# One-hot rows of the retrieval layer: second key index by one comparison for 8 tokens, gate moved to the first index

## What is computed

```
q = (hf @ wq).reshape(n, 8, 2, 64)
s = einsum('nhpd,hpkd->nhpk', q, subkeys)            # 8 heads, 2 halves, 128 keys each
sv, si = top_k(s, 16)
cand = sv[:, :, 0, :, None] + sv[:, :, 1, None, :]   # 16 x 16 sums per head
top_v, top_pos = top_k(cand, 16)
experts = si0 * 128 + si1 at top_pos                 # 8 x 16 = 128 experts of 16384 per token
gates = softmax(top_v)
act = gelu(einsum('td,tkd->tk', xb, u[experts]))
y = einsum('tk,tkd->td', gates * act, v[experts])
```

## Time and profile before

| what | value |
|---|---|
| median of 3 runs | 3950.86 us (3949.44 to 3951.46) |
| profiled execution, span from first to last instruction | 3944.0 us |
| busy: PE / PE weight load / DVE / ACT / POOL | 3668.8 / 2099.9 / 2582.7 / 732.8 / 1645.1 us |
| granted TensorE clock, mean | 0.972 |

### The profile page before, as it was taken

One profiled execution on the slowest core, in us unless ns is written; L12 is line 12 of the kernel. 1 busy time (PEld: TensorE's weight loads), 2 busy tenths in 40 slices (PEclk: granted clock), 3 DMA queues, 4 the chain that ended last, 5 costly groups with the idle time before them and its releaser, 6 DMA issues. The chain is left out here.

```text
span 3944.0 us, 39966 instructions
## 1 busy us (share of the span) xinstructions
PE 3668.8 (93%) x13726; PEld 2099.9 (53%) x13726; DVE 2582.7 (65%) x5929; ACT 732.8 (19%) x1622; POOL 1645.1 (42%) x1498
## 2 busy tenths in 40 slices
PE   2988888999999999999989887889999999999997
PEld 1545676655555555555445566765555555555543
DVE  5685688777666666677724738878677646556344
ACT  1143355400000000000012535552000000000000
POOL 0030155446556644444502003544777655445340
PEclk7998999999999999999999998999999999999999
DMA  6321234579999999999930131447999999989774
GB/s 218 126 101 46 90 86 145 185 289 405 379 379 369 378 373 378 379 372 353 393 138 2 47 121 54 126 136 256 359 410 410 387 354 354 366 337 359 304 290 160
DMA packets 365386, 1026.96 MB, mean 260 GB/s; under 512 B 30849, under 2 KB 132481, under 8 KB 364417
## 3 DMA queue, kind: packets, MB, share of 16 engines
q0 software_dynamic: 147456, 536.94, 35.5%
q1 hardware_dynamic: 118000, 433.99, 28.9%
q10 hardware_dynamic: 99728, 53.48, 4.8%
HBM read 965.07 MB, written 59.22 MB: 260 GB/s over the span
## 5 line engine op out<-in xcount | busy, mean ns | idle before, releaser
L1859 PE MATMUL ps<-colsT,arena 128*128 128x384 f32 x4096 | 1359.0, 486 | 5.6 <-DMA arena<-in_peer_ut 5.6
L1859 PEld LDWEIGHTS ps<-colsT,arena 128*128 128x128 f32 x4096 | 775.8, 190 | 584.4 <-issue 94.7
L1894 PE MATMUL ps<-arena 128*128 128x512 f32 x1536 | 676.5, 592 | 0.0
L1366 POOL DMA_INDIRECT proj<-in_peer_u,eidx x336 | 478.9, 1425 | 240.9 <-DVE modbc L1560 110.5
L1366 POOL DMA_INDIRECT proj<-in_peer_v,eidx x335 | 361.1, 1078 | 312.7 <-DVE colsT L1571 214.5
L1894 PEld LDWEIGHTS ps<-arena 128*128 128x128 f32 x1536 | 291.8, 190 | 345.2 <-issue 317.6
L1352 POOL TENSOR_SCALAR x<-iota,modbc 128x128 f32<-128x128 f32 x192 | 145.2, 771 | 719.3 <-ACT modbc L1692 551.5
L1560 DVE CUSTOM_DVE_ANT_0 proj<-proj,rows 128x1024 f32<-128x1024 f32 x336 | 399.4, 1222 | 59.0 <-DMA proj<-in_peer_u,eidx 57.2
L1571 DVE SCALAR_TENSOR_TENSOR colsT<-proj,modbc,colsT 128x1024 f32<-128x1024 f32 x330 | 410.1, 1286 | 14.4 <-DMA proj<-in_peer_v,eidx 13.1
L1894 PE MATMUL ps<-arena,rows 128*128 128x512 f32 x768 | 337.8, 592 | 0.0
L1894 PE MATMUL ps<-arena,x 128*128 128x512 f32 x768 | 337.7, 592 | 0.0
(11 more groups left out here) (298 smaller groups left out, 3716.3 us busy)
## 6 DMA issues: line engine op xcount, KB each, us to landing
arena<-in_peer_ut SPq DMA_DIRECT2D x256, 512.0 KB
arena<-in_peer_v SPq DMA_DIRECT2D x256, 512.0 KB
gmat_d<-arena ACTq DMA_DIRECT2D x24, 2048.0 KB, 9.3
arena<-gmat_d SPq DMA_DIRECT2D x64, 768.0 KB
proj<-in_w_adaT SPq DMA_DIRECT2D x48, 512.0 KB
modbc<-in_w_adaT SPq DMA_DIRECT2D x30, 512.0 KB, 3.7
rows<-in_w_adaT SPq DMA_DIRECT2D x18, 512.0 KB, 3.5
arena<-in_w_in SPq DMA_DIRECT2D x2, 4224.0 KB, 16.6
```

The lines of the kernel that those rows point to most:

```text
L1366: pool.indirect_dma_start(ring[slots[at]], None, tab, bass.IndirectOffsetOnAxis(ap=eidx[:, b * SLOTS + q:b * SLOTS + q + 1], axis=0)).then ...
L1859: mm = pe.matmul(ps[:, 2 + j % 2, 0:ND], utab[:, j % UR, k], hT[:, k, NG:T], start=(k == 0), stop=(k == KT - 1))
L1894: mm = pe.matmul(ps[:, Y_BANKS[2 * d + c2], :], wT[j % CR][:, d * P:(d + 1) * P], vtab[:, j % VR, c2 * 512:(c2 + 1) * 512], start=(j == 0) ...
```

## The change

B is made by one tensor_tensor per 8 tokens (iota against j, both broadcast, is_equal), without the gate. The gate goes into A: on POOL the tensor_scalar becomes (iota equal i) times gate, with two per-partition scalars; on ACT the Abs gets scale -1 and the Relu becomes four instructions of 128 columns, relu(gate - 2|i - iota|), because its bias now differs per token. `turned_out` is one instruction of 384 columns and a wait of ACT for its own result. The waits count in sets of 8 tokens.

```
-                        pool.tensor_scalar(agrp[n % A_GRP][:, t], iota128[:, :], ijgT[:, d % 2, 0, 4 * q + t:4 * q + t + 1], 0.0,
-                                           ALU.add, ALU.is_equal).then_inc(p_made, 1)
+                        tok = 4 * q + t
+                        pool.tensor_scalar(agrp[n % A_GRP][:, t], iota128[:, :], ijgT[:, d % 2, 0, tok:tok + 1],
+                                           ijgT[:, d % 2, 2, tok:tok + 1], ALU.is_equal, ALU.mult).then_inc(p_made, 1)
...
-                    for t in range(16 * step, 16 * step + 16):
+                    for t in range(16 * step, 16 * step + 16, B_SET):
                         n = d * P + t
-                        if n >= B_TOK and t % 4 == 0:
-                            dve.wait_ge(g_mm, (n - B_TOK) // 4 + 1)
-                        dve.tensor_scalar(bring[:, n % B_TOK], iota128[:, :], ijgT[:, d % 2, 1, t:t + 1],
-                                          ijgT[:, d % 2, 2, t:t + 1], ALU.is_equal, ALU.mult).then_inc(b_made, 1)
+                        if n >= B_TOK:
+                            dve.wait_ge(g_mm, (n - B_TOK + B_SET) // 4)
+                        dve.tensor_tensor(bring[:, n % B_TOK:n % B_TOK + B_SET],
+                                          iota128[:, :].unsqueeze(1).to_broadcast([P, B_SET, NKEY]),
+                                          ijgT[:, d % 2, 1, t:t + B_SET].unsqueeze(2).to_broadcast([P, B_SET, NKEY]),
+                                          ALU.is_equal).then_inc(b_made, 1)
...
-                    c.link(act.activation(ijgT[:, d % 2, 0], ps[:, 0, 0:P], ACT.Copy, scale=-1.0))
-                    act.activation(ijgT[:, d % 2, 1:3].rearrange("p a t -> p (a t)"), ps[:, 0, P:3 * P], ACT.Copy).then_inc(tr_out, 1)
+                    act.activation(ijgT[:, d % 2].rearrange("p a t -> p (a t)"), ps[:, 0, 0:3 * P], ACT.Copy).then_inc(tr_out, 1)
+                    act.wait_ge(tr_out, d + 1)
...
                     for t in range(4):
-                        c.done(act.activation(four[:, t], iota128[:, :], ACT.Abs, bias=ijgT[:, d % 2, 0, 4 * q + t:4 * q + t + 1]))
+                        tok = 4 * q + t
+                        c.done(act.activation(four[:, t], iota128[:, :], ACT.Abs, scale=-1.0, bias=ijgT[:, d % 2, 0, tok:tok + 1]))
                     c.wait()
-                    act.activation(four, four, ACT.Relu, scale=-1.0, bias=1.0).then_inc(a_made, 1)
+                    for t in range(4):
+                        tok = 4 * q + t
+                        act.activation(four[:, t], four[:, t], ACT.Relu, scale=-2.0,
+                                       bias=ijgT[:, d % 2, 2, tok:tok + 1]).then_inc(a_made, 1)
...
                         if act_marks(n):
-                            pe.wait_ge(a_made, n // 2 + 1)
+                            pe.wait_ge(a_made, 4 * (n // 2) + 4)
...
-                        pe.wait_ge(b_made, 4 * n + 4)
+                        pe.wait_ge(b_made, 4 * n // B_SET + 1)
```

More of the change, by code:

```diff
@@ L43 @@
 UR, VR, GR = 3, 3, 3
-A_GRP, B_TOK = 4, 16
+A_GRP, B_TOK, B_SET = 4, 16, 8
 ADA_RING = 5
@@ L1688, in turned_out @@
                     if d >= 2:
-                        act.wait_ge(b_made, (d - 1) * P)
+                        act.wait_ge(b_made, (d - 1) * (P // B_SET))
                         act.wait_ge(p_made, (d - 1) * (P // 2))
-                    c.link(act.activation(ijgT[:, d % 2, 0], ps[:, 0, 0:P], ACT.Copy, scale=-1.0))
-                    act.activation(ijgT[:, d % 2, 1:3].rearrange("p a t -> p (a t)"), ps[:, 0, P:3 * P], ACT.Copy).then_inc(tr_out, 1)
+                    act.activation(ijgT[:, d % 2].rearrange("p a t -> p (a t)"), ps[:, 0, 0:3 * P], ACT.Copy).then_inc(tr_out, 1)
+                    act.wait_ge(tr_out, d + 1)
                 def mark_rows(n):
```

## The result

| what | before | after |
|---|---|---|
| median of 4 runs | 3950.15 us (3945.36 to 3951.46) | 4005.41 us (3998.52 to 4009.72) |
| ratio, with its 95% interval | | 1.0138 (1.0124 to 1.0152) |
| profiled execution: its span | 3944.0 us | 4003.3 us (its time 4005.1) |
| busy PE / DVE / ACT / POOL | 3668.8 / 2582.7 / 732.8 / 1645.1 us | 3695.2 / 2484.4 / 793.6 / 1722.1 us |
| granted clock, mean | 0.972 | 0.965 |

The change costs 55 us. I had forecast 33 and slower, with 4005 inside the range. The direction holds; 22 us are missing from the sum.

A forecast was written before the change was run, and what follows sets the result against it. The dense loop is TensorE's, and the head's idle time there is mainly ScalarE's chain. Relus add 16.6 us a layer, 33 in two, other terms about 0: 3950.9 + 33 = 3984 us, range 3962 to 4020.

The forecast's parts named there:

- The gap is ScalarE's chain: PE's 1.18 us idle before group 3, steps 1 to 6: ended by ScalarE's mark between two copies, not VectorE.
- B by sets: VectorE making B by sets of 8: 98 us less VectorE work, 0 on the path.
- Relu by token: 0.62 per mark: ScalarE's four Relus for one: 0.62 us more per mark; blocks 6.4, 5.1, 5.1; 33 in two layers.
- POOL's second scalar: POOL's rows of A with one pointer more: taken as 0, bounds 0.71 to 0.85 us a row.
- POOL held by the sets: At a block's start VectorE's sets delay POOL's group 3 rows to 587.6, ScalarE's chain allows 587.4: tie, 0.
- The clock: Rival: gaps grown to 1.8 us lower PE's clock in half of 36 steps, 32 us more, 4016; chance 0.14.
- POOL's two signs: Expected signs: POOL's L1352 mean above 0.85 us, and no PE wait on it in steps 1 to 6.
- The sum's base: Profiled span 3944.0 plus 33 is 3977; median stands 6.9 above the span, so 3950.9 plus 33 is 3984.

The follow-up runs named there:

- after, again: The changed kernel itself, unaltered, run again beside the other kernels: 4002.99 us, ratio 1.0136.
- Relu by token, alone: Kernel before with only its Relu cut into four of 128 columns, each with a per-partition bias: 3993.12 us, ratio 1.0117.
- four Relus, immediate bias: Kernel before with its Relu cut into four of 128 columns, the bias an immediate: 3962.30 us, ratio 1.0039.
- sets alone: Kernel before with only B made by sets of 8 tokens, the gate left out altogether: 3955.63 us, ratio 1.0017.
- after, one Relu: Changed kernel with one 512-column Relu with immediate bias again, even groups without gate; POOL's second scalar kept: 3959.98 us, ratio 1.0033.
- before, marks later: Kernel before with ScalarE's mark of group n + 4 moved behind the copy of group n + 1: 3915.21 us, ratio 0.9918.
- after, marks later: Changed kernel with ScalarE's mark of group n + 4 moved behind the copy of group n + 1: 3956.40 us, ratio 1.0021.
- before, marks later, square first: Kernel before with marks behind copies and `square` and `root` ahead of the mark in block 1: 3908.24 us, ratio 0.9896.
- after, marks later, square first: Changed kernel with marks behind copies and `square` and `root` ahead of the mark in block 1: 3947.30 us, ratio 0.9998.

## Why the prediction was right, and where its size was off

PE in the six blocks of both layers, worked out from the views by stretch of each profile (length, busy, the rest) and, in the last column, from the granted clock: (1 - mean) / 0.5 of the length is the time at 1.2 GHz. The stretches end some 0.2 us later in each layer than those above. Each row is one execution; the changed kernel's two differ by 4 us in busy time and 10 in the last column.

```
kernel                          length   busy   idle   at 1.2 GHz, us
before                           573.8  479.9   93.9   72
after                            625.4  498.1  127.3  113
after, again                     628.6  502.5  126.2  123
Relu by token, alone             615.0  489.9  125.1   96
four Relus, immediate bias       584.8  477.9  106.8   61
sets alone                       581.2  481.4   99.8   75
after, one Relu                  586.7  483.5  103.2   82
before, marks later              540.2  474.3   65.9   75
after, marks later               583.6  486.0   97.6  102
before, marks later, square first 531.2  472.7   58.5   72
after, marks later, square first  572.5  484.0   88.5   89
```

The split has a limit. A run of matmuls counts as busy to its modelled end, so work cut into more runs counts as longer: at a block's start groups 0 and 1 now run apart, 2.05 and 2.08 us for the 3.75 of the earlier trace rows, some 2 us of the 18 in six blocks; and two runs of eight at 1.13 became one of sixteen at 2.02 where the marks stand later.

- *The gap is ScalarE's chain.* Right, and shown three ways: it grew by what the Relus' handing on grew (0.64 and 0.27), taking 98 us of work off VectorE left it at 1.18, and moving the mark closed it.
- *B by sets: 98 us, 0 on the path.* Right. VectorE's wait for exps at the end of block 2 grew as its cover, from 6.45 us to 8.12:

```profile
697.16 0.29 DVE L1453 TENSOR_REDUCE proj<-proj 128x8 f32<-128x128 f32 x1 [8.12 <-ACT proj L1679]
```

- *Relu by token: 0.62 per mark; blocks 6.4, 5.1, 5.1.* Right in size: 0.64, and idle time per block 5.9, 5.3, 5.6. An operand per partition costs 93 ns here (390 against 297). The Trainium skill (ScalarE: Activation LUTs, section "What ACT_TABLE_LOAD costs") has the same 93 ns, and its figures had given 0.65 per mark. That the idle time of the whole change is 33.4 against the sum's 33 is in part luck. The Relus alone give 31.2. The sets with POOL's second scalar, which the sum had at 0, give 9.3 by themselves (103.2 less 93.9), and on top of the Relus only 2.2, which fits the start of a block, where the longer marks and POOL's rows run beside each other.
- *POOL's second scalar: taken as 0.* Wrong, inside its bounds. Four rows beside nothing last 3.11 us after, 0.78 each, where the same view before has 2.80 to 2.95, some 0.70 to 0.74. It is 0.04 to 0.08 a row.
- *POOL held by the sets: a tie, 0.* The mechanism is right, the tie was lost by 0.9 us a start. I had counted two holds in the first eight rows; there are three. Start of block 2, POOL, VectorE, PE and ACT, against the earlier trace rows:

```profile
592.41 0.33 PE L1876 MATMUL ps<-ident,proj 128*128 128x128 f32 x1 [1.82 <-DVEq L1458]
...
593.52 2.36 DVE L1521 TENSOR_TENSOR x<-iota,modbc 128x1024 f32<-128x1024 f32 x2 [1.22 <-ACT modbc L1694]
...
593.59 5.20 POOL L1353 TENSOR_SCALAR x<-iota,modbc 128x128 f32<-128x128 f32 x4 [12.46 <-ACT modbc L1694]
...
598.77 4.16 POOL L1353 TENSOR_SCALAR modbc<-iota,modbc 128x128 f32<-128x128 f32 x4
...
598.84 2.08 PE L1892 MATMUL ps<-x 128*128 128x128 f32 x8 [0.58 <-POOL x L1353]
...
601.03 1.24 DVE L1521 TENSOR_TENSOR x<-iota,modbc 128x1024 f32<-128x1024 f32 x1 [2.04 <-PE ps L1892]
601.45 0.57 ACT L1723 ACTIVATE arena<-ps 128x512 f32<-128x512 f32 x1
...
602.99 1.33 PEld L1892 LDWEIGHTS ps<-x,modbc 128*128 128x128 f32 x8 [0.66 <-POOL modbc L1353]
```

  Here the label is right: POOL's second four end at 602.93 and PE's weight load goes at 602.99. ScalarE's copy of group 1 ended at 602.02, 0.9 earlier and 9.6 after the turn, which is what my chain gave (9.7). The rows 5.20 and 4.16 are 2.09 and 1.05 over the undisturbed 3.11: two holds, and a third from the set at 601.03. Group 3 starts some 10.6 us after the turn, 8.3 before. By the experiments this term, the second scalar, the new `turned_out` and what hangs on them are the 11 us of the changed kernel with one Relu.
- *The clock: taken as 0, and as a rival of 0.14 at 4016.* **This is the term that failed.** PE's busy time rose by 18.2 us, and the clock of all first-layer blocks fell by more than the 0.02 that I had named as the sign of it (the second layer's by 0.02, 0.01 and 0). The time at 1.2 GHz rose by 41 us, and at half speed that can add some 20 to the busy time. Two rows of block 2 after, scores and a group, timeline of PE:

```profile
617.10 3.52 PE L1853 MATMUL ps<-proj 64*128 64x128 f32 x32
...
658.29 1.96 PE L1892 MATMUL ps<-x,modbc 128*128 128x128 f32 x8 [1.82 <-POOL x L1353]
```

  The scores take 2.06 us at the full clock, the eight matmuls 1.13. Both rows stand just behind a gap of 1.82. Busy time by stretch, block 2 from 25 us behind its turn to its end, the kernel before and the kernel after:

```profile
602.72:672.06 69.34, 60.30 (x324) 43.78 (x324) 56.38 (x235) 38.40 (x86) 33.78 (x40) 1.00 0.58 171
617.41:698.12 80.71, 68.46 (x368) 51.21 (x364) 49.38 (x183) 47.12 (x122) 47.99 (x45) 0.94 0.51 150
```

  The record of the granted clock in the traces shows where. In blocks 2 and 3 of both layers, past the first 12 us of a block, the clock is never at 1.2 GHz in the kernel before, nor with four Relus with an immediate bias, nor in the changed kernel with one Relu, nor in the kernel before with the marks later. It falls to it 5 times in the kernel after, 7 times in its second profile and 5 times with the Relu by token alone, and each of the 17 stretches begins within 1.4 us of the end of a gap of 1.82. The rival was right in kind and too large: it had half of 36 steps, and in these blocks 5 to 7 of 24 gaps did it. The five of the kernel after are 17 of the 41 us; 17 more lie in block 1 and 8 at the starts of blocks 2 and 3.
- *POOL's two signs.* L1353's mean is 1.05 to 1.09, above the 0.85 stated. PE's waits on it in steps 1 to 6 are there by name, but are ScalarE's, as shown above; of the six below, five are such gaps of 1.82 and the sixth, 0.58 at the block's start, is POOL's own. The list of waits of PE in block 2 (total, times, longest):

```profile
PE ps L1892 <- POOL x L1353: 9.7, 6, 1.8
```

- *The sum's base.* The profiled span stood 6.9 us under the median before; after, it stands 2.1 under. The profile before is of a somewhat quick run, so part of the profiles' 59 is the difference between executions; the forecast of 3984 goes by the median and isn't touched by it. Of the 52 us that the blocks grew by, 33 are idle time and 18 busy time (32 and 23 in the second profile).

**What stays open.** That a gap of 1.8 brings the clock down in some steps is seen behind the 17 gaps above; why behind these and not the others isn't. The low time in block 1 is not explained: it rose from 41 to 58 us, but it is 61 also in the changed kernel with the marks later, whose waits there are other ones, up to 5.9 us past the first. That kernel also has one low stretch within block 2, behind three waits of 0.45, 1.13 and 0.59 us. Closing the gap of 1.18 brought no clock back (75 and 72 us against 72), so in these kernels gaps of that length had cost none.

Partly open is why the two kernels stay 39 to 41 us apart once the marks are behind the copies. Of the 43.4 and 41.3 us in length between them in the table, 31.7 and 30.0 are idle time, 11.7 and 11.3 busy time. Some 15 of the idle time are PE's waits for POOL's rows (15.5 against 0.8), and 2.4 are the longer first marks of blocks 2 and 3 (3.25 against 2.65, four times). Of the other 15 or so, 8 lie in block 1, which lasts 109.7 against 101.2, and 103.0 against 96.6 with `square` first. I ran no kernel that takes POOL's hold away by itself.

## What to carry to other kernels

When a change relieves one engine by giving work to another, price the instructions added to the engine in the chain, at the spacing that neighbours of the same form show, and give the relieved engine's time no value unless its own wait is short: 98 us off VectorE bought nothing here, 0.64 us on ScalarE in each step's chain and at the starts cost 44 us. Before believing the name in a wait, look at which row ends just ahead of the waiter; here the label said VectorE, then POOL, and in the steps it was ScalarE, until the marks were moved and POOL's name came true. On a chain of copies with other work between them, try moving that work behind the second copy first: it took 31.5 us off with the same instructions, and 39 with `square` and `root` moved too.

## What the runs showed of the hardware

- An operand per partition costs ScalarE 93 ns in an ACTIVATE of 128 columns (390 against 297), and 0.09 us in the spacing of four in a row (0.29 against 0.20).
- VectorE's sets hold POOL, and hardly the other way: two sets in a row last 2.36 us beside POOL, 1.23 for one, while POOL's four rows beside them go from 2.79 to 4.88. The Trainium skill (SBUF — State Buffer, section "SBUF: two separate sides") has the exclusion, for a VectorE instruction with two SBUF inputs and a GpSimd one that reads SBUF; the runs agree with it, and 2.09 us for two sets is near the full length of both.
- Longer idle time of PE came with a lower clock, but not at every length: in the kernel after 33 us more idle with 18 more busy, with the Relus alone 31 with 10, and with four short Relus, whose gap is 1.45, 13 with none. In blocks 2 and 3 of these kernels, past a block's start, the clock fell only behind gaps of 1.82 (5 to 7 of 24 in a profile), and behind none of 1.18 or 1.45.
